# Gate logits by seven block products for eight, joined by adding DMAs

## The reference

```python
h = rms_norm(x, g_mix) * (1.0 + sc1) + sh1
(a_q, a_k, a_v, conv_in, c_q, c_k, c_v, c_r, c_low, d_q, d_k, d_v, gate_logits) = jnp.split(h @ w_in, split_points, axis=-1)
y_a = dilated_attention_mixer(...) @ w_br_a
y_b = conformer_conv_mixer(...) @ w_br_b
y_c = gla_mixer(...) @ w_br_c
y_d = stick_breaking_mixer(...) @ w_br_d
gates = jax.nn.sigmoid(gate_logits).reshape(bsz, seq, 4, D_MODEL)
merged = gates[:, :, 0] * y_a + gates[:, :, 1] * y_b + gates[:, :, 2] * y_c + gates[:, :, 3] * y_d
x = x + gt1 * (merged @ w_out)
```

## Time and profile before

| | us |
|---|---|
| median of 3 executions | 1984.47 (1983.59 to 1989.29) |
| the profiled execution | 1990.35 |
| its span | 1988.6 |
| TensorE busy | 1927.7 (97%) |
| VectorE busy | 1191.7 (60%) |
| ScalarE busy | 831.3 (42%) |
| GpSimd busy | 227.2 (11%) |

### The profile page before, as it was taken

How to read it: one execution, slowest core, us unless ns; L and a number is a source line. 1 busy time by engine, 2 the same in 40 slices (tenths; PEclk the granted TensorE clock), 3 DMA queues, 4 the chain that set the end, 5 groups by cost and what they waited for, 6 DMA issues and landing times. The chain is left out here.

```text
span 1988.6 us, 24178 instructions
## 1 busy us (share of the span) xinstructions
PE 1927.7 (97%) x9224; PEld 1551.3 (78%) x9224; DVE 1191.7 (60%) x1555; ACT 831.3 (42%) x1314; POOL 227.2 (11%) x136
## 2 busy tenths in 40 slices
PE   5999999999999999998999999999999999999999
PEld 4787888878766667876788788788788887888887
DVE  6545757101256666727657478667766765678855
ACT  5411111223466633164656255333455445444443
POOL 0121121211121225212101000000000000000000
PEclk9999999999999999999999999999999999999999
DMA  8345554323311242244122576501353546963343
GB/s 268 109 142 152 154 164 133 100 86 111 129 56 48 64 166 67 94 175 161 51 87 71 167 259 221 190 11 39 110 164 128 170 149 217 318 201 108 98 118 101
DMA packets 229004, 266.24 MB, mean 134 GB/s; under 512 B 12010, under 2 KB 157546, under 8 KB 228890
## 3 DMA queue, kind: packets, MB, share of 16 engines
q1 hardware_dynamic: 228720, 264.63, 42.0%
q10 hardware_dynamic: 170, 0.07, 0.0%
HBM read 187.46 MB, written 77.20 MB: 133 GB/s over the span
## 5 line engine op out<-in xcount | busy, mean ns | idle before, releaser
L663 PE MATMUL dn_ps<-h_hi,dn_hi 128*128 128x512 f32 (+1 forms) x1120 | 453.5, 405 | 16.0 <-ACT dn_out L156 5.1
L665 PE MATMUL dn_ps<-h_hi,dn_lo 128*128 128x512 f32 (+1 forms) x1120 | 440.2, 393 | 0.0
L664 PE MATMUL dn_ps<-h_lo,dn_hi 128*128 128x512 f32 (+1 forms) x1120 | 439.9, 393 | 0.0
L663 PEld LDWEIGHTS dn_ps<-h_hi,dn_hi 128*128 128x128 f32 (+1 forms) x1120 | 210.9, 188 | 84.2 <-issue 33.7
L156 ACT ACTIVATE dn_out<-dn_ps 128x512 f32<-128x512 f32 (+1 forms) x138 | 81.7, 592 | 424.1 <-PE dn_ps L665 402.8
L139 POOL TENSOR_TENSOR dn_lo<-dn_raw,dn_hi 128x1024 fp32r<-128x1024 f32 (+1 forms) x69 | 172.3, 2498 | 663.8 <-ACT dn_hi L135 663.8
L665 PEld LDWEIGHTS dn_ps<-h_hi,dn_lo 128*128 128x128 f32 (+1 forms) x1120 | 210.5, 188 | 47.9
L664 PEld LDWEIGHTS dn_ps<-h_lo,dn_hi 128*128 128x128 f32 (+1 forms) x1120 | 210.9, 188 | 43.1 <-issue 1.2
L1227 ACT ACTIVATE tl_ring_hi<-tl_cell 128x512 fp32r<-128x512 f32 x112 | 70.6, 630 | 140.7 <-PE mg_ps_y L665 126.5
L664 PE MATMUL mg_ps_y<-tl_ring_lo,tl_ring_hi 128*128 128x512 f32 x320 | 124.6, 389 | 0.0
L663 PE MATMUL mg_ps_y<-tl_ring_hi,tl_ring_hi 128*128 128x512 f32 x320 | 124.6, 389 | 0.0
(11 more groups left out here) (420 smaller groups left out, 3719.1 us busy)
## 6 DMA issues: line engine op xcount, KB each, us to landing
dn_raw<-w_in_dram SPq DMA_DIRECT2D x70, 512.0 KB, 4.3
tl_raw_hidden<-hidden SPq DMA_DIRECT2D x112, 256.0 KB, 2.7
ada<-w_ada_dram SPq DMA_DIRECT2D x24, 1024.0 KB, 8.0
proj<-dn_out SPq DMA_DIRECT2D x72, 256.0 KB, 2.3
logits<-dn_out SPq DMA_DIRECT2D x64, 256.0 KB, 2.3
tl_unit<-w_up_dram SPq DMA_DIRECT2D x64, 256.0 KB, 3.2
hidden<-tl_hidden_sum SPq DMA_DIRECT2D x16, 1024.0 KB, 4.9
tl_cell<-w_down_dram SPq DMA_DIRECT2D x64, 256.0 KB, 5.1
```

Source lines behind the costliest of these rows:

```text
L663: nc.tensor.matmul(out, w_hi[:, t, :], x_hi[:, t, :], start=begin, stop=False, skip_group_check=reopened)
L664: nc.tensor.matmul(out, w_hi[:, t, :], x_lo[:, t, :], start=False, stop=False, skip_group_check=reopened)
L665: mm = nc.tensor.matmul(out, w_lo[:, t, :], x_hi[:, t, :], start=False, stop=end, skip_group_check=reopened)
```

## The change

A new class, `Gates`, takes the gate columns over. They are paired: columns of gates 2g and 2g + 1 with the same n form a pair b, 16 in all. With the features halved (kh) and the tokens halved, each pair is a product of 2 x 2 by 2 x 2 blocks, done by seven products M1 to M7 of half the features instead of eight. A product is 12 matmuls (4 triples).

- **Weight sums.** M3, M5, M6 and M7 take sums of weight blocks. POOL issues 32 DMAs of 1 MB between places in DRAM (16 copies, 16 that add), 16 in the front, 16 in stick-breaking, into `gate_sums`.
- **Token sums.** In the front, behind the convolution's taps, DVE makes nine differences of 128x2048 and four low parts, ACT four high parts. Three blocks (6 MB with both parts) are stored to `gate_tokens`; at the front's end ACT and DVE copy two blocks over parts of `h_hi` and `h_lo`, where the last front tile has taken its token halves in the other order.
- **Two phases.** In phase one (q from 0 to 47: M1, M6, M7) the three products of a pair go on summing in the same bank, which is stored after each. Then SP loads the six parts of the token blocks over the rest of `h_hi` and `h_lo`. In phase two (q = 48 to 111: M2, then M5, M4, M3) each product is joined to what lies in `logits` by a DMA from POOL that adds (`add`).
- **The weight tiles** are 256 KB each, four cells, product q + 4 loaded when product q's place in `move` comes.
- The gates of odd number come out negated, and the sigmoid takes a scale of -1.
- **Counts**: stick-breaking 34 products, linear attention 39, window 32, close 7. ACT has a split behind each copy; in phase two POOL has an add for each product between its low parts.

The core of the diff:

```diff
+class Gates:
...
+    OUTPUTS = {M1: ((0, 0),), M6: ((0, 1),), M7: ((1, 0), (1, 1)), M2: ((0, 0),), M5: ((1, 1),), M4: ((1, 0),), M3: ((0, 1),)}
+    REOPENED = (M6, M7, M3)
+    FIRST = 3 * PAIRS
+    SECOND = FIRST + PAIRS
+    COUNT = 7 * PAIRS
...
+        self.products = [(p, b) for first in range(0, self.PAIRS, 2) for p in (self.M1, self.M6, self.M7) for b in (first, first + 1)]
+        self.products += [(self.M2, b) for b in range(self.PAIRS)]
+        self.products += [(p, b) for b in range(self.PAIRS) for p in (self.M5, self.M4, self.M3)]
...
+        self.sums = [(kind, g, r) for kind in ("copy3", "copy2", "add3", "add2") for g in range(2) for r in range(2)]
+        self.early_sums = len(self.sums)
+        self.sums += [(kind, g, r) for kind in ("copy1", "copy4", "add1", "add4") for g in range(2) for r in range(2)]
...
+    def load(self, sp, q):
...
+            sp.wait_ge(self.lo_ready, q - self.CELLS + 1)
+        p, b = self.products[q]
...
+        sp.dma_start(self.cell(self.dense.raw, q), self.block(p, b)).then_inc(self.loaded[q % self.CELLS], 16)
...
+    def run(self, pe, triples):
+
+        while self.triple < triples:
...
+                pe.wait_ge(self.lo_ready, q + 1)
...
+                    pe.wait_ge(self.copied, q - 1)
+                if q == self.SECOND:
+                    pe.wait_ge(self.tokens_in, 16 * 6)
...
+    def copy(self, act, q):
+        act.wait_ge(self.done, q + 1)
...
+            self.wait_stored(act, q - 2)
+        self.nc.scalar.activation(self.dense.out[:, q % 2, :], self.dense.ps[:, q % 2, :], ACT.Copy).then_inc(self.copied, 1)
+
+    def serve(self, act, products):
+
+        while self.served < products:
+            self.copy(act, self.served)
+            if self.served + self.CELLS < self.COUNT:
+                self.split(act, self.served + self.CELLS)
+            self.served += 1
+
+    def add(self, pool, q):
+
+        p, b = self.products[q]
+        place, = self.OUTPUTS[p]
+        before = self.place[{self.M2: self.M1, self.M3: self.M6, self.M4: self.M7, self.M5: self.M7}[p], b]
+        pool.wait_ge(self.copied, q + 1)
+        self.wait_stored(pool, before)
+        self.nc.gpsimd.dma_start(self.out_at(b, place), self.dense.out[:, q % 2, :], accum_op=ALU.add).then_inc(self.added_in[q % 2], 16)
+
+    def lower(self, pool, products, added):
+
+        lows = min(products + self.LEAD, self.COUNT)
+        while self.lowered < lows or self.added < added:
+            if self.added < added and (self.added + self.CELLS <= self.lowered or self.lowered >= lows):
+                self.add(pool, self.added)
+                self.added += 1
+            else:
+                if self.lowered % 2 == 0 and self.sum_at < len(self.sums):
+                    self.sum_step(pool)
+                self.low(pool, self.lowered)
+                self.lowered += 1
+
+    def move(self, sp, products):
+
+        while self.moved < products:
+            q = self.moved
+            if q + self.CELLS < self.COUNT:
+                self.load(sp, q + self.CELLS)
+            if q < self.FIRST:
+                p, b = self.products[q]
+                sp.wait_ge(self.copied, q + 1)
+                for place in self.OUTPUTS[p]:
+                    sp.dma_start(self.out_at(b, place), self.dense.out[:, q % 2, :]).then_inc(self.stored[q % 2], 16)
+            if q == self.FIRST:
+                sp.wait_ge(self.done, self.FIRST)
+                for block, p in ((self.T1, self.M5), (self.T4, self.M4), (self.B22, self.M3)):
+                    for part, rows in enumerate((self.k.h_hi, self.k.h_lo)):
+                        sp.dma_start(self.view(rows, p).bitcast(F32), self.k.gate_tokens[block, part]).then_inc(self.tokens_in, 16)
+            self.moved += 1
...
+    HIGH_AFTER = {29: (0,), 30: (1, 2), 32: (3,)}
+    SUMS_AT = (8, 9, 10, 11, 12, 13, 14, 15, 18, 20, 22, 24, 27, 29, 31, 33)
...
+                if j in SUMS_AT:
+                    gates.sum_step(pool)
...
+            low_difference(T2)
+            low_difference(T4)
...
+            dve.wait_ge(dense.done, NH * (N_TILES - 1) + 1)
+            nc.vector.tensor_copy(gates.view(k.h_lo, gates.M6), t_lo[T2][:, :, :])
+            nc.vector.tensor_copy(gates.view(k.h_lo, gates.M7), t_lo[T3][:, :, :])
...
+                nc.scalar.activation(logits_at(m), logits_at(m), ACT.Sigmoid, scale=1.0 if m % 2 == 0 else -1.0).then_inc(gate_ready, 1)
...
-    HEAD, PREPARE, DURING, MERGING = 3, 8, 6, 4
...
+    HEAD, PREPARE, DURING, MERGING = 2, 14, 11, 7
...
-    PREPARE, LEVEL, STATE, NORM = 8, 7, 2, 5
-    HEAD = 6
+    FROM = dense.gates.triple // 4
+    PREPARE, STATE, NORM = 14, 3, 9
+    HEAD = 4
     PAIRS = N_CH // 2
     GROUPS = (LEVELS + 1) * PAIRS
+    SCORED = [PREPARE]
+    for j in range(LEVELS + 1):
...
+            dense.triples(pe, 2 * HEAD)
             pe.wait_ge(low_in, 32)
             for c in range(2):
                 for h in range(NH):
                     last = nc.tensor.matmul(pre_bank(c)[:, h, :], wg[:, c * P:(c + 1) * P], low[:, h * HALF:(h + 1) * HALF], start=True, stop=True)
             last.then_inc(pre_done, 1)
-            dense.pieces(pe, HEAD - 3)
+            dense.triples(pe, 2 * HEAD)
             pe.wait_ge(v_in, 16)
...
-            dense.serve(act, FROM + 1)
+            dense.serve(act, FROM + HEAD // 2)
...
+                dense.serve(act, FROM + LEVEL + STATE + h + 1)
...
-    HEAD, EACH = 6, 2
+    FROM = dense.gates.triple // 4
...
-        HALVES = (HEAD + EACH * (N + LAG - 1)) // 3
+        GATES = HEAD + N + LAG - 1 + LAST_GATES
...
-                    dense.pieces(pe, 1)
+                    dense.triples(pe, 2)
...
-            dense.serve(act, FROM + 1)
+            dense.serve(act, FROM + HEAD)
```

More of the change, by code:

```diff
@@ L95, in __init__ @@
         window = [(t * P, P, t) for t in range(R_CONV)]
-        gates = [(COL_GATES + i * D + n * P, P, None) for n in range(D // P) for i in range(4)]
-        self.tiles = conv + stick + low + linear + window + gates
+        self.tiles = conv + stick + low + linear + window
         self.early = len(conv)
-        self.first_gate = len(self.tiles) - len(gates)
-        self.piece, self.served, self.lowered, self.moved = 0, 0, 0, 0
+        self.first_gate = len(self.tiles)
+        self.gates = Gates(nc, k, self, w_in)
     def use_extra(self, raw, hi, lo):
@@ L159, in store, with triples, serve, lower @@
         column, width, row = self.tiles[j]
[L160 to L164 removed]
+        half = self.tokens(j, h)
+        dest = self.k.proj[row * P:row * P + width, half * HALF:(half + 1) * HALF]
         sp.wait_ge(self.copied, NH * j + h + 1)
         sp.dma_start(dest, self.out[0:width, h, :]).then_inc(self.stored[h], 16)
[L168 to L207 removed]
+    def triples(self, pe, count):
+        self.gates.run(pe, self.gates.triple + count)
+    def serve(self, act, products):
+        self.gates.serve(act, products)
+    def lower(self, pool, products):
+        self.gates.lower(pool, products, products if products == Gates.COUNT else products - 1)
+    def move(self, sp, products):
+        self.gates.move(sp, products)
     def finish(self, sp, tiles):
@@ L349, in _, with store_tokens @@
             late = 0
+            def store_tokens(block, hi, lo):
+                for part, rows in enumerate((hi, lo)):
+                    sp.dma_start(k.gate_tokens[block, part], rows.bitcast(F32)).then_inc(t_stored, 16)
             for j in range(dense.SLOTS, N_TILES + 2):
-                dense.load(sp, j)
+                if j < N_TILES:
+                    dense.load(sp, j)
+                else:
+                    for q in range(2):
+                        gates.load(sp, 2 * (j - N_TILES) + q)
                 if late < LATE and load_step(late) == j:
@@ L373, in _ @@
                                     base=0, pattern=[[-1, P]], channel_multiplier=1).then_inc(const_ready, 1)
[L374 removed]
+            for j in range(OPENING, N_TILES):
+                if j in SUMS_AT:
+                    gates.sum_step(pool)
                 dense.low(pool, j)
+            for q in range(2):
+                gates.low(pool, q)
         @block.scalar
@@ L438, in _ @@
                     dense.copy(act, j, 1)
-                    dense.split(act, j + 2)
+                    if j + 2 < N_TILES:
+                        dense.split(act, j + 2)
+                    else:
+                        for q in range(2):
+                            gates.split(act, q)
+                for i in HIGH_AFTER.get(j, ()):
+                    act.wait_ge(t_step, (3, 5, 7, 9)[i])
+                    if i == T3:
+                        act.wait_ge(t_stored, 16 * 4)
+                    nc.scalar.activation(t_hi[i][:, :, :], t_full[i][:, :, :], ACT.Copy).then_inc(t_hi_ready, 1)
                 if j == SQUARE_AFTER:
@@ L639, in _ @@
                 modulation(OPEN_CHUNKS + i)
+            for n in range(1, 10):
+                difference(n)
+            low_difference(T1)
```

(13 more changed lines are left out.)

334 lines of the change are left out of this document (221 added, 113 removed).

## The result

The changed kernel takes 2082.7 us (median of 4, 2081.6 to 2083.9) where the kernel before takes 1986.3: 96 us slower, ratio 1.0485 with a 95% interval of 1.0466 to 1.0504. The forecast was 1988.5, with a range from 1952 to 2015.

The account below looks back on a forecast made before the run. TensorE, busy 1927.7 of 1988.6 us, was taken as the bound, so matmul count and gaps matter. Stage terms +1 - 5 + 10 - 3 + 1 = +4 us on the 1984.5 us median gave 1988.5 us, range 1952 to 2015.

Parts of the forecast that it names:

- The saving, -43.5: All stages after the front: 192 fewer matmuls at 0.2267 us each save 43.5 us as the ideal.
- Linear attention, +10: Linear attention: -13.6 saved, +14 for a blocked first split, +3 behind token tiles, +7 in the normalisation; bounds -12 to +25.
- Window, -3: Window: -10.9 saved, +4 for a later first split, +4 for ACT's extra copies and splits; bounds -11 to +6.
- The adds, 0: Phase two: POOL's adding DMAs land within about 4.8 us and stay hidden between products, so they cost nothing.
- Rival B: Phase two, in the window's tail and close: adds land late, from 5.5 us on, giving 2005 to 2035; chance 0.15.
- ACT's extra 55 us: Three stages and close's start: more copies (+28.4 us) and half-size splits (+27 us) on ACT.
- POOL's low parts, 0: POOL: 112 half-size low parts at 1.25 us each, +60 us of work, run ahead and cost nothing.
- stick-breaking, -5: Stick-breaking: -16.3 saved, 7 given back at the start and 4 in the steps; bounds -16 to +5.
- Close, +1: Close: -2.7 saved, +4 for seven products' splits and adds on its queues; bounds -3 to +8.
- The signs: Linear attention: PE gap 8 to 11 us, level scores 9 later; stick-breaking 3 to 7 shorter; adds under 5 us.
- rival A: Whole kernel: the saving stays because give-backs shrink to a third, giving 1955 us (1945 to 1970); chance 0.28.
- rival C: Three stages: their chains, not PE's filling, set the ends; no saving and 20 us more, 2005 us; chance 0.07.

Follow-up runs that it names:

- experiment 15: The kernel before with 21 matmuls instead of 24 in each gate half, 192 fewer in all, nothing added: 1967.0 us (0.9901).
- experiment 3: The changed kernel with POOL's 64 DMAs of phase two overwriting instead of adding: 2067.0 us.
- experiment 5: The changed kernel with weight tile loads two products earlier and POOL's DMAs of phase two overwriting instead of adding: 2009.5 us.
- experiment 14: The kernel before with 96 more copies of 128x512 on ACT, some 57 us: 1998.9 us (1.0054).
- experiment 4: The changed kernel without the 32 weight-sum DMAs and their waits, those products taking unsummed weight blocks: 2075.2 us.
- experiment 16: The kernel before with both 21 matmuls a gate half and 96 more copies on ACT: 1976.0 us (0.9950).
- experiment 6: The changed kernel with loads two products earlier, and weight sums, token block loads and adding left out: 1997.0 us (1.0055).
- experiment 13: As experiment 6, but stores write a constant tile, so that ACT's copies wait for no store: 1999.0 us.
- experiments 8: The changed kernel with loads two products earlier, all sums in the front, token loads spread, phase one's stores issued by ACT: 2006.2 us.

## Why the prediction was wrong

The prediction failed by size in one term, the saving, and by a wrong lead in another: it took the lead of a weight tile as four products, 10.9 us, where ACT wants the tile after one, 2.72 us.

- **The saving, -43.5.** The step "192 x 0.2267" was right as PE work and wrong as time: experiment 15 gives 18.5. The text said itself that a product taken away counts only if the chain beside it is shorter, and then entered the full figure for each stage and took single give-backs off.
- **Linear attention, +10; measured +56.** The blocked first split was right in place: it was forecast at some 20 us after the stage's first copy, with the stage's activations at 22. The split started 16.7 us after that copy (731.22 - 714.50), and the activations came at 22.7 because two more splits waited 3.2 us together; that 22 and 22.7 agree so well is in part luck. The first level scores came 10.6 us later behind the first copy than before (67.8 for 57.2 us), for 9 forecast. The levels then take 85.9 us for 75.7, with the wait of 18.05 us behind the token tiles in them, where 3 us were forecast. The normalisation was put at 7 us for nine copies and nine splits in place of five and two; the stage's tail, from the first square at 894.86 to the window's first load, takes 71.7 us where it was 36.4 (866.51 to 902.92). The step that failed is the lead of the loads. The prediction wrote "a lead of four products, 10.9 us", which is the distance to PE's use of the tile. ACT splits it right behind the copy of the product at whose place it was loaded, so the lead is one product, 2.72 us. That made the waits behind bursts longer than I priced them, and for every load outside a burst I priced nothing, though the nearest rows (2.3 us in the median for 256 KB, up to 13.5) left 0.4 us of margin under 2.72, and the tiles took 3.9 to 4.3. The 6 MB of token tiles at 408 GB/s are 15.4 us, too, not the 18 that I wrote. With the loads two products earlier 53.5 us come back.
- **Window, -3; measured +20.** The same step, here behind bursts: the first split starts 13.5 us after the stage's first copy (2.4 before), where 4 more were forecast, and all 34.5 us of the stage's waits for tiles are waits of 9 us and more. With the loads early it takes 219.2 us, as before (218.7).
- **The adds, 0; measured about 20.** I set the landing at the store's 2.3 us. It is 4.3 in the median (3.9 to 9.0), inside the 4.8 that I called hidden, and still costs 15.7 us (experiment 3) to 19.7 (experiment 5). Rival B had the adds as a cost, with a chance of 0.15, but neither the landing (5.5 us and more) nor the place (the window's tail and close; without the adding linear attention is 9 us shorter and the window 6). With the loads early ACT's waits for landings do carry the cost (55.8 to 37.8 us). In the changed kernel ACT waited only 5.8 us for landings, so there a part must act in another way: ACT's waits for weight tiles fell from 165.6 to 155.4 us without the adding. POOL's issue, 0.88 us for 0.56 in the plain form, was not tried apart. That DVE holds the adds, as rival B supposed, does not show: from 1010 to 1046 us, with DVE busy all the time, they land in 3.9 to 4.3 us, and from 872 to 896, with DVE busy for 3.6 of 24 us, in 4.0 to 7.1. Which of these DVE operations run in a two-port mode no row shows, so the Trainium skill's rule (SBUF — State Buffer, "Who interferes with whom") is neither shown nor refuted here. The Trainium skill's fit for a POOL-issued DMA (DMA: Bandwidth & Descriptors, "Anatomy of one DMA"), an estimate of 2.6 us for 256 KB, agrees with the 2.5 us of the plain form; the adding form lands 1.8 us later.
- **ACT's extra 55 us** were charged with 4 + 4 us and part of the 7; experiment 14 gives 12 for about the same amount (56 us). This was about right.
- **POOL's low parts, 0.** They take 1.60 us in the mean, not 1.25. PE waits 4.6 us for them in all, so this was nearly right.
- **Front, +1; measured 0**, and **stick-breaking, -5; measured +7**. Without the sums it takes 194.7 us (experiment 4), 10 less, which is close to the forecast: that POOL's copies "share the transfer" was the right mechanism, but it was given a part of 7 us.
- **Close, +1; measured +9.** With the loads early it is +7 (873.6 us). What the rest is was not tried; the kernel before with fewer matmuls or more work on ACT (experiments 14 to 16) also shows 869 to 870 us for 867.
- **The signs.** The late level scores, a weight tile behind the token tiles (17.2 us to land) and adds under 5 us in the median came. PE's gap at linear attention's start was 5.8 us, not 8 to 11, and stick-breaking got longer. PE's waits for ACT's copies of gate products, 59.2 us for 5.1 before, were rival B's sign; with the loads early they are 34.3, so a good part of them came from the late tiles.
- The prediction's **rival A** (the saving stays) is refuted, by 128 us. Its **rival C** (the chains set the ends) had the right idea for 25 of the 43.5 us.

The account, from the kernel before to the changed one: -18.5 (matmuls) + 9 (ACT's work) + 21 + 12.5 (sums and token loads) + 20 (adding) + 53.5 (late loads) = +97.5, for 96.4 measured. It has to come out so, because each term is the difference of two neighbouring kernels on one path from the old to the new; that it does is no evidence. The terms with experiment 15 in them are uncertain by some 6 us. The 21 us between experiment 16 (1976.0) and experiment 6 (1997.0) stay open. They hold tiles of half the size loaded in the same bursts, ACT's splits behind them, POOL's low parts, logits written twice, and PE's shorter lead over ACT; experiment 13 rules out the landing of stores by itself, and nothing tells the others apart. The traces show the place: linear attention takes 205.0 us in 6 and 191.4 in 16, stick-breaking 191.7 and 196.9. Of those 13.6 us, 9 are there at the first activation of the stage's own chain, 17.0 us after the stage's first load in 6 and 8.0 in 16: with the loads early too, ACT must first serve three products, of which a store or a tile stands behind the 4 MB (experiments 8 and 13). The parts were measured in one order, so the shares of the overlapping ones would be a little different in another.

## What to carry to other kernels

A smaller unit of work shortens the time between the issue of its load and its use, even if nothing else moves. Here the tile's bytes were halved and its work quartered (12 matmuls for 48), so the lead fell from 10.9 to 2.72 us. Set the lead of a load in microseconds against its landing time, not in units, and measure it to the engine that wants the tile first. Before counting a saving on a filler, take the work out of the old kernel and time it; here that one kernel said 18.5 instead of 43.5. And on a queue that carries loads behind stores, look for circles: a load behind a store that waits for the chain that the load feeds costs its landing each round (3 us of wait in each head here; read from the rows, and gone with the loads early, but not tried apart).

## What was not expected of the hardware

A DMA that adds 256 KB from SBUF to DRAM lands in 4.3 us in the median, the same DMA without adding in 2.5. POOL is held for about 0.9 us by issuing one (862 to 1227 ns), and for 0.56 us (539 to 642 ns) by the plain one. Low parts on POOL of half the size take 1.60 us in the page's mean where the larger took 2.46, so halving the tile did not halve them in the mean. The longest ones, 2.9 to 5.4 us, all fall where DVE is busy from their start to their end; with DVE idle most take 1.25 to 1.29 us, a few 1.59 to 1.90. What makes them long was not tried. Groups of instructions, changed kernel:

```profile
L184 POOL TENSOR_TENSOR dn_lo<-dn_raw,dn_hi 128x512 fp32r<-128x512 f32 x112 | 178.9, 1600 | 143.1 <-ACT dn_hi L180 142.9
...
L333 POOL TENSOR_TENSOR dn_lo<-dn_raw,dn_hi 128x1024 fp32r<-128x1024 f32 (+1 forms) x37 | 90.8, 2455 | 313.3 <-ACT dn_hi L329 313.3
...
L230 POOL DMA_DIRECT2D logits<-dn_out x64 | 58.5, 913 | 208.0 <-ACT dn_out L213 207.8
```
